# The first projection of a hybrid decoder step: transfers in order of need, two units interleaved by tile, low halves on VectorE

## What is computed

```python
h = rmsnorm(x, p['norm_mix_g'][0])
u, v = jnp.split(jax.nn.gelu(h @ w_in + b_in), 2, axis=-1)     # w_in: (1024, 2048)
v = layernorm(v, ln_g, ln_b)
...
def rmsnorm(x, g):
    y = xf * lax.rsqrt(jnp.mean(xf * xf, axis=-1, keepdims=True) + EPS)
    return y.astype(x.dtype) * g
```

## Time and profile before

| | us |
|---|---|
| median of 3 runs | 1571.55 |
| the runs | 1569.86 to 1572.32 |
| span of the profiled execution | 1568.3 |
| its own time | not listed apart from the runs |
| TensorE busy in that span | 1520.0 (97%), 10354 matmuls |
| VectorE, ScalarE, GpSimd busy | 803.9, 735.4, 1087.2 |

### The profile page before, as it was taken

How to read it: one execution, slowest core, us unless ns; L and a number is a source line. 1 busy time by engine, 2 the same in 40 slices (tenths; PEclk the granted TensorE clock), 3 DMA queues, 4 the chain that set the end, 5 groups by cost and what they waited for, 6 DMA issues and landing times.

```text
span 1568.3 us, 32552 instructions
## 1 busy us (share of the span) xinstructions
PE 1520.0 (97%) x10354; PEld 1481.2 (94%) x10354; DVE 803.9 (51%) x1787; ACT 735.4 (47%) x1406; POOL 1087.2 (69%) x1044
## 2 busy tenths in 40 slices
PE   5999999999999999999999999999899999999998
PEld 5999999998999999888999999999788889999997
DVE  4455555116545412997645521666667776554401
ACT  5655443345444435556544434557534424444332
POOL 5657878774877678985776767766645656767674
PEclk9999999999999999999999999999999999999998
DMA  5434445453444655222556455544412125444453
GB/s 196 148 113 153 144 159 162 136 137 106 154 154 147 164 149 175 83 80 73 163 163 167 135 139 145 186 131 143 128 39 83 60 92 172 159 151 145 125 151 109
DMA packets 87678, 212.48 MB, mean 135 GB/s; under 512 B 25424, under 2 KB 33136, under 8 KB 87472
## 3 DMA queue, kind: packets, MB, share of 16 engines
q1 hardware_dynamic: 87600, 211.49, 44.0%
HBM read 201.80 MB, written 9.66 MB: 135 GB/s over the span
## 4 chain that ended last, share of the span: by engine, by line
PE 91%; DVE 5%; issue 2%; ACT 1%; DMA 1%; POOL 1%; DVEq 0%; SPq 0%; POOLq 0%; ACTq 0%
PE bank L871 26%; PE bank L873 26%; PE bank L872 26%; PE bank L1226 2%; PE bank L1087 2%; PE bank L1248 1%; PE bank L1237 1%; DVE ssq L1875 1%; PE bank L1286 1%; PE bank L1140 1%; POOL M L701 0%; DVE bank L2149 0%; DMA raw<-in_a_in 0%; PE bank L1316 0%; DMA fst<-in_d_st 0%
## 5 line engine op out<-in xcount | busy, mean ns | idle before, releaser
L595 POOL TENSOR_TENSOR wlo<-raw,whi 128x512 fp32r<-128x512 f32 (+3 forms) x400 | 460.6, 1151 | 381.6 <-ACT whi L1379 344.3
L871 PE MATMUL bank<-Gh,whi 128*128 128x320 f32 x1928 | 603.1, 313 | 19.7 <-DVE Gl L1864 15.8
L873 PE MATMUL bank<-Gh,wlo 128*128 128x320 f32 x1928 | 596.6, 309 | 0.0
L872 PE MATMUL bank<-Gl,whi 128*128 128x320 f32 x1928 | 596.4, 309 | 0.0
L597 POOL TENSOR_TENSOR wlo<-raw,whi 128x512 fp32r<-128x512 f32 (+2 forms) x400 | 481.3, 1203 | 0.0
L1379 ACT ACTIVATE whi<-raw 128x1024 fp32r<-128x1024 f32 (+3 forms) x400 | 374.9, 954 | 49.2 <-PE bank L873 38.6
L871 PEld LDWEIGHTS bank<-Gh,whi 128*128 128x128 f32 x1928 | 362.6, 188 | 23.9 <-issue 15.3
L872 PEld LDWEIGHTS bank<-Gl,whi 128*128 128x128 f32 x1928 | 362.9, 188 | 1.1
L873 PEld LDWEIGHTS bank<-Gh,wlo 128*128 128x128 f32 x1928 | 362.6, 188 | 0.0
L871 PE MATMUL bank<-Hh,whi 128*128 128x320 f32 x912 | 283.6, 311 | 4.0 <-DVE Hl L2090 2.5
L873 PE MATMUL bank<-Hh,wlo 128*128 128x320 f32 x912 | 281.8, 309 | 0.0
(11 more groups left out here) (372 smaller groups left out, 1814.9 us busy)
## 6 DMA issues: line engine op xcount, KB each, us to landing
raw<-in_f_up SPq DMA_DIRECT2D x176, 512.0 KB, 3.4
raw<-in_f_down SPq DMA_DIRECT2D x64, 384.0 KB, 3.2
raw<-in_f_down SPq DMA_DIRECT2D x64, 320.0 KB, 3.2
raw<-in_c_pw SPq DMA_DIRECT2D x24, 512.0 KB, 3.6
raw<-in_a_in SPq DMA_DIRECT2D x16, 512.0 KB, 3.6
raw<-in_d_qk SPq DMA_DIRECT2D x16, 512.0 KB, 3.7
raw<-in_d_vg SPq DMA_DIRECT2D x16, 512.0 KB, 3.6
raw<-in_a_out SPq DMA_DIRECT2D x8, 512.0 KB, 3.5
```

Of the source, the lines that this page charges most:

```text
L595: pool.tensor_tensor(wlo[k][:, 0:half], raw[k][:, 0:half], whi[k][:, 0:half].bitcast(F32), ALU.subtract).then_inc(half_ready, 1)
L871: nc.tensor.matmul(dst, wh, h, start=start and n == 0, stop=False)
L872: nc.tensor.matmul(dst, wh, lo, start=False, stop=False)
L873: ins = nc.tensor.matmul(dst, wl, h, start=False, stop=stop and end and n == len(tiles) - 1)
```

## The change

Only the start of phase `a_in` is touched.

- SyncE: the order is unit 0, X tiles 0 and 1, the 72 columns of gains, unit 1, X tiles 2 to 4, X tiles 5 to 7, units 2 and 3, the rest of par, units 4 to 7, then the three tables.
- ScalarE: a square root of one number first; high part of unit 0, Gh 0 and 1, high part of unit 1, Gh 2 to 7, high part of unit 2, squares 0 to 3, high part of unit 3, squares 4 to 7, high parts of units 4 and 5. The loop over n makes its first high part (unit 6) at n = 4.
- VectorE: the low parts of units 0 and 1, four halves, alternating with Gl 0 to 2; then Gl 3 to 7; then the sums, whose running value lies in a PSUM bank.
- GpSimd: waits for both low parts, then makes units 2 to 7, then the masks, then unit 8 on.
- TensorE: twelve products of `ones` with itself (128 columns, full float32) into a bank that is overwritten later; units 0 and 1 interleaved by tile; unit 2; the norm's product; units 3 to 8, each waiting for the eviction of the unit four before it.

```diff
@@ -41,6 +41,7 @@
 POOLW = (2, 4, 8, 16)
+XPARTS = ((0, 2), (2, 5), (5, 8))
 CHUNK = 64
...
@@ -398,8 +400,10 @@
         def _(sp):
-            sp.dma_start(par[:, :], t["par"]).then_inc(par_in, 16)
-            sp.dma_start(X[:, :], t["x"]).then_inc(x_in, 16)
+            def load_x(i):
+                a, z = XPARTS[i][0] * NT, XPARTS[i][1] * NT
+                sp.dma_start(X[:, a:z], t["x"][:, a:z]).then_inc(x_in[i], 16)
@@ -476,9 +480,19 @@
                 if name == "a_in":
+                    gain = 9 * KT
+                    load(name, l, 0, 0)
+                    load_x(0)
+                    sp.dma_start(par[:, 0:gain], t["par"][:, 0:gain]).then_inc(gain_in, 16)
+                    load(name, l, 0, 1)
+                    load_x(1)
+                    load_x(2)
+                    load(name, l, 0, 2)
+                    load(name, l, 0, 3)
+                    sp.dma_start(par[:, gain:NCOL], t["par"][:, gain:NCOL]).then_inc(par_in, 16)
                     for k in range(SLOTS):
-                        load(name, l, 0, k)
-                    first = 1
+                        load(name, l, 1, k)
+                    first = 2
                     sp.dma_start(wsT, t["a_wsT"]).then_inc(mix_in, 16)
@@ -765,9 +779,11 @@
                 if name == "a_in":
-                    for k in range(4):
-                        split_lo(k, k, w)
-                    first = 1
+                    pool.wait_ge(half_ready, 2)
+                    pool.wait_ge(lo_ready, 2)
+                    for k in range(2, 8):
+                        split_lo(k, k % 4, w)
+                    first = 2
@@ -874,9 +890,9 @@
-            def in_unit(u, k, ready=None):
-                if not isinstance(u, int) or u > 2:
-                    pe.wait_ge(evac, u - 2)
+            def in_unit(u, k, ready=None, held=2):
+                if not isinstance(u, int) or u > held:
+                    pe.wait_ge(evac, u - held)
                 unit(u, k, Gh, Gl, acc[k][:, 0:NT], range(KT), ready=ready)
@@ -1015,9 +1031,31 @@
-            first_body("a_in", 0, 0)
-            for n in range(4, 9):
-                in_unit(n, n % 4)
+            def first_units():
+                pe.wait_ge(consts, 1)
+                for _ in range(12):
+                    nc.tensor.matmul(mixb[0][:, 0:P], ones[:, :], ones[:, :], start=True, stop=True)
+                for kt, m in [(0, 0), (1, 0), (0, 1), (1, 1)] + [(kt, m) for kt in range(2, KT) for m in range(2)]:
+                    if kt == 0:
+                        pe.wait_ge(hi_ready, m + 1)
+                        pe.wait_ge(half_ready, m + 1)
+                    if kt == KT // 2:
+                        pe.wait_ge(lo_ready, m + 1)
+                    pe.wait_ge(g_ready, kt + 1)
+                    h, lo, dst = tile_of(Gh, kt), tile_of(Gl, kt), acc[m][:, 0:NT]
+                    wh, wl = tile_of(whi[m], kt, P), tile_of(wlo[m], kt, P)
+                    nc.tensor.matmul(dst, wh, h, start=kt == 0, stop=False)
+                    nc.tensor.matmul(dst, wh, lo, start=False, stop=False)
+                    ins = nc.tensor.matmul(dst, wl, h, start=False, stop=kt == KT - 1)
+                    if kt == KT - 1:
+                        ins.then_inc(unit_done, 1)
+            first_units()
+            in_unit(2, 2)
+            norm_stat(0)
+            for n in range(3, 9):
+                in_unit(n, n % 4, held=3)
             v_mean()
@@ -1501,12 +1539,36 @@
-            act.wait_ge(par_in, 16)
+            def first_hi(m):
+                for i, (a, z) in enumerate(XPARTS):
+                    if m == a:
+                        act.wait_ge(x_in[i], 16)
+                nc.scalar.activation(tile_of(Gh, m), tile_of(X, m), ACT.Copy, scale=col("gain", m)).then_inc(g_hi, 1)
+            def first_square(m):
+                if m >= 2:
+                    act.wait_ge(ssq_ready, m - 1)
+                nc.scalar.activation(sq[m % 2][:, 0:NT], tile_of(X, m), ACT.Square).then_inc(sq_ready, 1)
             act.wait_ge(consts, 2)
+            nc.scalar.activation(spare1[:, 0:1], eps[:, 0:1], ACT.Sqrt)
             split_hi(0, 16, 0, UNIT)
+            act.wait_ge(gain_in, 16)
+            first_hi(0)
+            first_hi(1)
             split_hi(1, 16, 1, UNIT)
-            for m in range(KT):
-                residual(0, m, m % 2, x_in, 16)
+            for m in range(2, KT):
+                first_hi(m)
+            split_hi(2, 16, 2, UNIT)
+            for m in range(4):
+                first_square(m)
+            split_hi(3, 16, 3, UNIT)
+            for m in range(4, KT):
+                first_square(m)
+            split_hi(4, 32, 0, UNIT)
+            split_hi(5, 32, 1, UNIT)
@@ -1542,9 +1604,11 @@
             for n in range(16):
-                ahead(0, 0, n, UNIT)
+                if n >= 4:
+                    ahead(0, 0, n, UNIT)
                 if n == 0:
                     std(stat_done, 1, std_ready)
+                    act.wait_ge(par_in, 16)
                 if n == 9:
@@ -1965,10 +2029,44 @@
+            def first_lo(u, half):
+                if half == 0:
+                    dve.wait_ge(hi_ready, u + 1)
+                a, z = half * UNIT // 2, (half + 1) * UNIT // 2
+                vec.tensor_tensor(wlo[u][:, a:z], raw[u][:, a:z], whi[u][:, a:z].bitcast(F32),
+                                  ALU.subtract).then_inc((half_ready, lo_ready)[half], 1)
+            def first_gl(m):
+                dve.wait_ge(g_hi, m + 1)
+                vec.scalar_tensor_tensor(out=tile_of(Gl, m), in0=tile_of(X, m), scalar=col("gain", m),
+                                         in1=tile_of(Gh, m).bitcast(F32), op0=ALU.mult,
+                                         op1=ALU.subtract).then_inc(g_ready, 1)
+            def first_sum(m):
+                run = mixb[2][:, 0:NT]
+                dve.wait_ge(sq_ready, m + 1)
+                if m == 0:
+                    vec.tensor_copy(run, sq[0][:, 0:NT]).then_inc(ssq_ready, 1)
+                else:
+                    dve.wait_ge(ssq_ready, m)
+                    vec.tensor_tensor(ssq[:, :] if m == KT - 1 else run, run, sq[m % 2][:, 0:NT],
+                                      ALU.add).then_inc(ssq_ready, 1)
+            first_lo(0, 0)
+            first_gl(0)
+            first_lo(0, 1)
+            first_gl(1)
+            first_lo(1, 0)
+            first_gl(2)
+            first_lo(1, 1)
+            for m in range(3, KT):
+                first_gl(m)
+            for m in range(KT):
+                first_sum(m)
             dve.wait_ge(par_in, 16)
-            dve.wait_ge(x_in, 16)
-            for m in range(KT):
-                residual(0, m, m % 2, m == 0)
```

More of the change, by code:

```diff
@@ L201, in trunk_kernel @@
         hist_ready, tail_ready = sem("history_ready"), sem("tail_ready")
-        par_in, x_in, fst_in, mix_in = sem("par_in"), sem("x_in"), sem("fst_in"), sem("mix_in")
+        par_in, fst_in, mix_in = sem("par_in"), sem("fst_in"), sem("mix_in")
+        gain_in, x_in = sem("gain_in"), [sem(f"x_in{i}") for i in range(len(XPARTS))]
         consts = sem("consts")
```

## The result

The changed kernel takes 1561.06 us in the median of four runs (1560.17 to 1562.96), the kernel before 1571.93 (four runs). The ratio is 0.9941, its interval 0.9928 to 0.9953: 9.3 us faster, between 7.4 and 11.3 (the two medians alone differ by 10.9). The profiled execution, the fastest of the four, took 1560.17, with a span of 1558.4 where 1568.3 stood, 9.9 less. In a second measurement, five runs beside eleven of the kernel before (medians 1561.94 and 1570.64), the ratio was 0.9936, from 0.9923 to 0.9949. Forecast was 1559.0 and a gain of 12.5: the time lies inside the range, the gain was too large by more than the measurement leaves open.

The account below looks back on a forecast made before the run. TensorE's stream bounds the end, so the gain lies before it is dense: 8.2 + 6.2 + 24.6 + 0.54 + 0.48 + 0.1 put unit 8's eviction at 40.1 instead of 52.56, 12.5 us less: time 1559.0, range 1556.8 to 1562.3.

Parts of the forecast that it names:

- T0: Start of unit 1's first product, from which TensorE's stream was to be dense; put at 8.2 us.
- the norm's chain: First standard deviation: squares and sums done at 16.8, norm's product behind unit 2 wanted at 18.1, so no cost.
- the sum: Front up to unit 8's eviction: T0, tiles, seven units, norm, first products and wait, together 40.1 instead of 52.56.
- the wait at unit 4: TensorE at unit 4, first to need an eviction (unit 0's, at 22.2): 0.1 wait, 0.24 for the product after.
- rival 3: VectorE slowed beside GpSimd: Gl 3 to 7 at 1.38 each, 2.7 us lost, 1561.7; chance 0.05.
- rival 4: TensorE's low clock level lasts some 19 us of dense work: no measurable change, 1568.5 to 1571.5; chance 0.03.
- rival 5: Low clock level for longer, units 0 to 6, 3.5 us a unit: slower, time passes 1574.7; chance 0.02.
- rival 6: Throwaway products hold back the first real one: 1.2 us on tile 0, still 1559.0; held in the forecast's 0.62.
- the same sum reads: DMA queue: landings in the new order from the old order's bytes per time; weights 0 at 4.1, weights 1 at 6.2.
- rival 2: First transfers share the engines: weights 0 and 1 land 1 us later, T0 9.2, 1560.0; chance 0.13.
- Fourteen tiles at 0.44: TensorE's dense work on units 0 and 1 from T0, at the high clock level: 6.2 us.
- rival 1: Clock low at T0: 3.6 us of dense work at 0.27 a product costs 1.8, gain 10.7, 1560.8; chance 0.15.

Follow-up runs that it names:

- the other one: The changed kernel itself, unedited, profiled again in a second measurement: that run 1564.11 us, median of five runs 1561.94, ratio to the kernel before 0.9936.
- With the gaps filled: Changed kernel with 18 throwaway products ahead instead of 12, and two more after each of unit 0's tiles 0 and 1: median 1558.79 us, ratio 0.9926.
- the kernel with the old wait: Changed kernel with units 3 to 8 again waiting for the eviction of the unit three before: 1563.26 us, kernel before 1571.76.
- the kernel with the same landing: Changed kernel without the twelve throwaway products, weights 1 landing at 8.2 as in the unit-by-unit kernel: 1563.16 us, kernel before 1569.07.
- X whole: Changed kernel with X as one transfer between unit 0's weights and the gains: 1564.24 us, kernel before 1569.07.
- the short transfers: Changed kernel with four more transfers of 72 columns of par behind the gains, ahead of unit 1's weights: 1563.61 us, kernel before 1569.22.

## Why the prediction was right and wrong

Right: where the gain comes from, and that it reaches the end; VectorE's 0.7 for a half (0.69); that the dense stream starts at T0 and TensorE then waits for no Gl; that the norm's chain and the masks are hidden; no table load ahead of the root. From the start of unit 2 to the eviction of unit 8 the sum had 25.5 us and the profile has 25.5; in part that is luck, since the wait at unit 4 and its first product took some 0.2 less than put, and the 0.2 from unit 8's products to its eviction weren't in the sum. Rivals 3, 4, 5 and 6 had nothing for them: the five Gl take 2.40 together and are done before GpSimd starts at 13.01, and the throwaway products end at 6.06, ahead of the first real one.

Two terms of the sum failed, and they are the whole of the difference, 2.4 us at the eviction of unit 8.

T0 was put at 8.2 and was 9.54. The step that failed is "the same sum reads": it took the bytes of the kernel before, slice by slice, for what the queue moves whatever is in it. By 7.5 us the kernel before had moved 2.16 MB and the changed one 1.72. The 1.41 MB up to weights 1, which the sum had moved at 5.6, had moved at 6.6, and the landing came 1.0 behind that, not 0.6 to 0.7: of the 1.4 us about 1.1 is rate and 0.3 the time to the landing. I took the value near the low end of its bound because three landings lay on one line, but these were landings of one order. The upper bound of 1 us, rival 2, was exceeded: weights 1 came 1.4 late in the profile and 2.6 late in the other one. At T0 that is 1.3 us.

Fourteen tiles at 0.44 were put at 6.2, with 0.24 for the first product, and took 7.45: 1.0. The step that failed is the high level taken for granted from T0 on, against rival 1, to which I gave 0.15: twelve throwaway products do raise the level, but then TensorE idles from 6.06 to 7.46 and works about half the time to 9.5, and in eight of the nine profiles with exactly twelve the level fell again ahead of the dense stream, for up to 6.8 us. With the gaps filled it didn't fall, in both profiles. The argument against it, that 5 us of work are more than the 3.6 that sufficed, speaks of rising and says nothing of falling. The Trainium skill, TensorE: Matmul & The Clock Gate, The HAM clock gate, has both directions: activity lifts the throttle, an idle stretch brings it back. The trace agrees on the first, and the kernel with the old wait on the second, behind its 3.40 us. The fall at the front of the changed kernel is not a plain case of it: in its two profiles no idle stretch ahead of it is longer than 1.4 us.

Rivals 1 and 2 together would have read 1559.0 + 1.8 + 1.0 = 1561.8, a gain of 9.7, and 1561.06 and 1561.94 were measured, gains of 9.3 and 10.1 by the ratios. They were priced one at a time.

The parts, each undone alone, by the eviction of unit 8 against the changed kernel's two profiles: the wider wait 1.9 to 3.9 (5.1 from T0, against fronts at the high level), the order of the transfers 1.7 to 3.6, the interleaving 0.8 to 2.7 (1.4 beside the kernel with the same landing). The halves on VectorE are worth 0.7 at T0 and between nothing and 1.8 at the eviction, the throwaway products 0 to 0.6 from T0. They don't add up to the gain exactly, each being worth what the others leave. The earlier table load and the place of the squares weren't undone alone, so what they bring isn't shown.

Open: why the queue moves 343 to 365 GB/s with nearly the same rows at 3 us and 400 at 9. The rate was higher with X in long rows (X whole, one profile), the short transfers cost 0.3 each at most; what else is in it, and the 1.2 us by which the landing of weights 1 differs between runs of the same order, wasn't settled. Also open is why the kernel with the old wait kept the high level at its front; its code is the changed kernel's up to there, so by what is on record it is a difference between runs.

## What to carry to other kernels

A sum of bytes taken from one order of transfers doesn't hold for another: price the landing that starts the dense stream from two sides, and leave more than a microsecond above it: here it came 1.4 and 2.6 late. Throwaway products must reach up to the dense work and into the gaps ahead of it, or what they raise is lost again before it is of use. A semaphore wait that is one unit too strict can cost as much as an order of transfers: 1.9 to 3.9 us here, against 1.7 to 3.6. And where the rest of the program differs by 3 us from run to run, an edit of the front is priced by a point just behind it, not by the end.

## What was not expected of the hardware

With the products ahead, the granted clock shows what the kernel before hid: it reads 0.50 at products 0.27 apart, while before the first rise the same spacing is shown with 1.00 (TensorE at 14 to 20 us in the kernel before). One idle stretch of 3.40 us behind the norm's product brought the low level too, and one of 2.15 to 2.17 us near 370 us brought it in ten profiles and not in three. And the time to a landing differs between runs of the same order: 5.4 to 6.6 us for the weights of unit 1.
